# Streaming expert weights in chunks of 2 MB instead of 1 MB, with four neighbouring rows to a partition

## The reference, cut to what matters

```python
def moe(x, w_router, b_router, w1, w3, w2):      # x: 256 tokens x 1024
    e_idx, gates = route(xf, w_router, b_router) # 2 of 16 experts for each token
    ...
    def expert_block(args):
        xb, e = args
        hb = jax.nn.silu(xb @ w1[e]) * (xb @ w3[e])   # w1, w3: 1024 x 1024
        return hb @ w2[e]                             # w2: 1024 x 1024
    ...
    out = jnp.zeros((t, d), x.dtype).at[tok_s].add(y) # weighted by the gate
```

## Time and profile before

| | us |
|---|---|
| median of 3 runs | 2483.45 (2482.26 to 2487.23) |
| the profiled execution, its time | 2489.44 |
| its span | 2487.8 |
| first layer of experts, first product to last | 178.7 to 613.0 |
| second layer of experts, first product to last | 783.1 to 1217.4 |

### The profile page before, as it was taken

The page is one execution under the profiler, slowest core; times in us unless marked ns, Lnnn a source line. Parts: engine busy times, 40 slices in busy tenths (PEclk is TensorE's granted clock), DMA queues, the critical chain, the costliest instruction groups (busy, mean ns, idle before and its releaser), DMA issues.

```text
span 2487.8 us, 30159 instructions
## 1 busy us (share of the span) xinstructions
PE 2232.2 (90%) x12373; PEld 1559.5 (63%) x12373; DVE 955.8 (38%) x1217; ACT 719.6 (29%) x896; POOL 68.1 (3%) x78
## 2 busy tenths in 40 slices
PE   8869999997866999999599987979989998897998
PEld 6544334332754343333299976769979997676998
DVE  4741000001673000000345557645545546754554
ACT  4621000001451000000333344243343334424332
POOL 2000000000000000000100010000000001000000
PEclk9979999999987999999899989789999999968999
DMA  7189999999439999999955542045545554304551
GB/s 258 37 361 423 425 424 424 423 425 417 163 126 383 425 424 424 424 424 425 333 190 185 177 133 94 1 139 186 185 136 187 186 178 141 101 1 136 176 183 64
DMA packets 194676, 618.56 MB, mean 249 GB/s; under 512 B 10360, under 2 KB 119040, under 8 KB 145408
## 3 DMA queue, kind: packets, MB, share of 16 engines
q1 hardware_dynamic: 192416, 612.01, 64.6%
q0 software_dynamic: 2144, 4.94, 0.8%
HBM read 615.86 MB, written 1.05 MB: 248 GB/s over the span
## 4 chain that ended last, share of the span: by engine, by line
PE 72%; DMA 12%; DVE 8%; ACT 3%; DVEq 2%; issue 2%; ACTq 0%; SPq 0%
PE W L1730 18%; PE W L1892 7%; PE W L1893 7%; PE W L1894 7%; DMA moe_own<-in_moe_w 5%; DMA moe_split<-in_moe_w 5%; PE acc L1620 4%; PE acc L1621 4%; PE acc L1624 4%; PE W L1585 4%; PE W L1586 4%; PE W L1587 4%; PE W L1714 2%; DMA moe_xt<-in_moe_w 2%; PE acc L1723 2%
## 5 line engine op out<-in xcount | busy, mean ns | idle before, releaser
L977 DVE TENSOR_TENSOR w_lo<-raw,w_hi 128x2048 fp32r<-128x2048 f32 (+2 forms) x216 | 466.6, 2163 | 473.4 <-ACT w_hi L633 472.0
L633 ACT ACTIVATE w_hi<-raw 128x2048 fp32r<-128x2048 f32 (+2 forms) x216 | 382.3, 1772 | 595.6 <-PE W L1894 320.6
L1892 PE MATMUL W<-xT_hi,w_hi 128*128 128x256 f32 x1408 | 401.2, 285 | 7.5 <-DVE xT_lo L997 7.5
L1893 PE MATMUL W<-xT_lo,w_hi 128*128 128x256 f32 x1408 | 400.6, 285 | 0.0
L1894 PE MATMUL W<-xT_hi,w_lo 128*128 128x256 f32 x1408 | 400.5, 284 | 0.0
L1228 DVE TENSOR_TENSOR hid<-W,hid 128x512 f32<-128x512 f32 x32 | 22.1, 692 | 735.6 <-PE W L1730 735.6
L1892 PEld LDWEIGHTS W<-xT_hi,w_hi 128*128 128x128 f32 x1408 | 270.2, 192 | 10.3 <-DVE xT_lo L997 8.9
L1893 PEld LDWEIGHTS W<-xT_lo,w_hi 128*128 128x128 f32 x1408 | 270.2, 192 | 1.6
L1894 PEld LDWEIGHTS W<-xT_hi,w_lo 128*128 128x128 f32 x1408 | 270.3, 192 | 0.0
L1585 PE MATMUL W<-w_hi,xT_hi 128*128 128x474 f32 (+1 forms) x400 | 155.3, 388 | 9.9 <-DVE w_lo L977 4.8
L1730 PE MATMUL W<-moe_split,xe 128*64 128x512 f32 x672 | 153.2, 597 | 9.5 <-DMA moe_split<-in_moe_w 8.2
(11 more groups left out here) (334 smaller groups left out, 2743.9 us busy)
## 6 DMA issues: line engine op xcount, KB each, us to landing
moe_own<-in_moe_w SPq DMA_DIRECT2D x120, 1024.0 KB, 26.2
moe_split<-in_moe_w SPq DMA_DIRECT2D x120, 1024.0 KB, 26.2
raw<-in_moe_w SPq DMA_DIRECT2D x108, 1024.0 KB, 25.8
raw<-in_ffn_w_gate SPq DMA_DIRECT2D x44, 1024.0 KB, 5.3
raw<-in_ffn_w_up SPq DMA_DIRECT2D x44, 1024.0 KB, 5.3
raw<-in_ffn_w_down SPq DMA_DIRECT2D x44, 1024.0 KB, 4.9
moe_xt<-in_moe_w SPq DMA_DIRECT2D x36, 1024.0 KB, 26.0
raw<-in_w_in SPq DMA_DIRECT2D x32, 948.0 KB, 4.9
```

The source lines that it names most:

```text
L633: s.activation(w_hi[split_slot(c)][:, 0:cols], raw[slot_of(c)][:, 0:cols], ACT.Copy).then_inc(hi_ready, 1)
L977: v.tensor_tensor(w_lo[split_slot(c)][:, 0:cols], raw[slot_of(c)][:, 0:cols], w_hi[split_slot(c)][:, 0:cols].bitcast(F32), ALU.subtract).t ...
L1892: t.matmul(out, hi, xT_hi[:, kc, :], start=(kc == 0), stop=False)
L1893: t.matmul(out, hi, xT_lo[:, kc, :], start=False, stop=False)
```

## The change

A chunk becomes 2 MB: 512 rows of a matrix, partition p holding rows 4p to 4p+3, one run of 16 KB. An expert has 6 chunks, a layer 96. The ring has 10 slots of 16 KB a partition over the same bytes: 3 `moe_split`, 3 `moe_own`, 3 `moe_raw` (each over two neighbouring raw slots, so its fill waits for the later of the two) and 1 `moe_xt`. PE counts a chunk as used after 8 products (16 records) instead of 4. The stationary operands of the gather and of the hidden transposes now take every fourth column of `x` and `hid` (a step of 16 bytes). The counts for which ACT and DVE wait are those of the same points of the work. In the changed kernel the lines stand three (PE's part) or four (SP's part) further down.

```diff
-MOE_CHUNKS = 12
+MOE_ROWS = 4
+MOE_Q = KC // MOE_ROWS
+MOE_CHUNKS = 3 * MOE_Q
...
-MOE_OWN = 6
+MOE_OWN = 3
 MOE_SPLIT_AT = 0
-MOE_OWN_AT = MOE_SPLIT_AT + 2 * SPLIT_SLOTS
+MOE_OWN_AT = MOE_SPLIT_AT + SPLIT_SLOTS
 MOE_RAW_AT = MOE_OWN_AT + MOE_OWN
-MOE_XT_AT = MOE_RAW_AT + RAW_SLOTS
-MOE_SLOTS = MOE_XT_AT + 2
+MOE_XT_AT = MOE_RAW_AT + RAW_SLOTS // 2
+MOE_SLOTS = MOE_XT_AT + 1
...
         def raw_freed(layer, i):
-            slot = MOE_RAW_AT + i
+            slot = MOE_RAW_AT + i // 2
...
                 def fetch(m):
-                    e, i, q = m // MOE_CHUNKS, m % MOE_CHUNKS // 4, m % 4
+                    e, i, q = m // MOE_CHUNKS, m % MOE_CHUNKS // MOE_Q, m % MOE_Q
                     slot = m % MOE_SLOTS
-                    dst = moe_ring[slot][:].rearrange("p (k n) -> p k n", k=2)
-                    src = A[(...)[i]][layer, e, 256 * q:256 * (q + 1), :].rearrange("(p k) n -> p k n", k=2)
+                    dst = moe_ring[slot][:].rearrange("p (k n) -> p k n", k=MOE_ROWS)
+                    src = A[(...)[i]][layer, e, MOE_ROWS * P * q:MOE_ROWS * P * (q + 1), :].rearrange("(p k) n -> p k n", k=MOE_ROWS)
                     sp.dma_start(dst, src).then_inc(moe_landed[slot], 16)
...
-                        i = m - MOE_RAW_AT
-                        sp.wait_ge(lo_ready, c_end - (c_end - 1 - i) % RAW_SLOTS)
+                        sp.wait_ge(lo_ready, max(c_end - (c_end - 1 - i) % RAW_SLOTS for i in (2 * (m - MOE_RAW_AT), 2 * (m - MOE_RAW_AT) + 1)))
...
-            def every_second(a, kc):
-                return a[:, 256 * (kc // 2):256 * (kc // 2 + 1)].rearrange("p (c k) -> p k c", k=2)[:, kc % 2, :]
+            def every_fourth(a, kc):
+                return a[:, 512 * (kc // 4):512 * (kc // 4 + 1)].rearrange("p (c k) -> p k c", k=MOE_ROWS)[:, kc % 4, :]
...
-                        last = t.matmul(W[:, bank, j * P:(j + 1) * P].rearrange("p (a t) -> p a t", a=2), every_second(x[:, b], kc),
+                        last = t.matmul(W[:, bank, j * P:(j + 1) * P].rearrange("p (a t) -> p a t", a=2), every_fourth(x[:, b], kc),
...
-                    last = t.transpose(W[:, 0, k * P:(k + 1) * P], every_second(hid, k), ident[:])
+                    last = t.transpose(W[:, 0, k * P:(k + 1) * P], every_fourth(hid, k), ident[:])
...
-                    for k in range(2):
-                        last = halves(bank, stationary, 2 * q + k, moe_ring[m % MOE_SLOTS], k * D)
+                    for k in range(MOE_ROWS):
+                        last = halves(bank, stationary, MOE_ROWS * q + k, moe_ring[m % MOE_SLOTS], k * D)
                     return last.then_inc(moe_used, 1)
```

More of the change, by code:

```diff
@@ L162, in sem @@
             return ctx.enter_context(nc.semaphore(name))
+        raw_base = place[0]
         raw = [at(f"raw{i}", [P, SLOT]) for i in range(RAW_SLOTS)]
@@ L258, in build_program, with over @@
         count_max = at("count_max", [P, 1])
[L259 to L263, removed]
+        own = [at(f"moe_own{i}", [P, MOE_ROWS * D]) for i in range(MOE_OWN)]
+        def over(name, n, offset):
+            return [nc.alloc_sbuf_tensor_at(f"{name}{i}", [P, MOE_ROWS * D], F32, offset=offset + i * MOE_ROWS * D * 4) for i in range(n)]
+        moe_ring = over("moe_split", SPLIT_SLOTS, split_base) + own + over("moe_raw", RAW_SLOTS // 2, raw_base) + over("moe_xt", 1, xt_base)
         ov_raw = own[0][:, 0:D]
@@ L431, in fetch @@
                 def fetch(m):
-                    e, i, q = m // MOE_CHUNKS, m % MOE_CHUNKS // 4, m % 4
+                    e, i, q = m // MOE_CHUNKS, m % MOE_CHUNKS // MOE_Q, m % MOE_Q
                     slot = m % MOE_SLOTS
-                    dst = moe_ring[slot][:].rearrange("p (k n) -> p k n", k=2)
-                    src = A[("moe_w1", "moe_w3", "moe_w2")[i]][layer, e, 256 * q:256 * (q + 1), :].rearrange("(p k) n -> p k n", k=2)
+                    dst = moe_ring[slot][:].rearrange("p (k n) -> p k n", k=MOE_ROWS)
+                    src = A[("moe_w1", "moe_w3", "moe_w2")[i]][layer, e, MOE_ROWS * P * q:MOE_ROWS * P * (q + 1), :].rearrange("(p k) n -> p k n", k=MOE_ROWS)
                     sp.dma_start(dst, src).then_inc(moe_landed[slot], 16)
@@ L464, in more_rounds @@
                                     sp.wait_ge(o["free"], N(KC * i + kc + 1, (r, 24 * NE), (e, 24)).v)
-                                    pair = w[256 * (kc // 2):256 * (kc // 2 + 1), :].rearrange("(p k) n -> p k n", k=2)
-                                    sp.dma_start(ov_raw, pair[:, kc % 2, :]).then_inc(o["landed"], 16)
+                                    four = w[512 * (kc // 4):512 * (kc // 4 + 1), :].rearrange("(p k) n -> p k n", k=MOE_ROWS)
+                                    sp.dma_start(ov_raw, four[:, kc % 4, :]).then_inc(o["landed"], 16)
             def ffn(c0, l, which):
@@ L762, in experts @@
                     one = NE * layer + e + 1
-                    act.wait_ge(moe_used, MOE_LAYER * layer + MOE_CHUNKS * e + 4)
+                    act.wait_ge(moe_used, MOE_LAYER * layer + MOE_CHUNKS * e + MOE_Q)
                     s.activation(gated[:], W[:, 0, :], ACT.Silu).then_inc(me["sg"], 1)
@@ L1225, in experts @@
                         softplus()
-                    dve.wait_ge(moe_used, MOE_LAYER * layer + MOE_CHUNKS * e + 8)
+                    dve.wait_ge(moe_used, MOE_LAYER * layer + MOE_CHUNKS * e + 2 * MOE_Q)
                     dve.wait_ge(me["sg"], one)
@@ L1704, in gather @@
                     for b in range(TB):
-                        last = t.matmul(W[:, 3, kc * CAP:(kc + 1) * CAP], every_second(x[:, b], kc),
+                        last = t.matmul(W[:, 3, kc * CAP:(kc + 1) * CAP], every_fourth(x[:, b], kc),
                                         chosen_tokens[:, b, 0:CAP], start=(b == 0), stop=(b == TB - 1))
@@ L1792, in experts @@
                     tokens = xe[e // 2 % 2][:, :, CAP * (e % 2):CAP * (e % 2 + 1)]
-                    for q in range(4):
+                    for q in range(MOE_Q):
                         chunk(m + q, 0, tokens, q)
@@ L1796, in experts @@
                             add_expert(e - 1)
-                    for q in range(4):
-                        chunk(m + 4 + q, 1, tokens, q)
+                    for q in range(MOE_Q):
+                        chunk(m + MOE_Q + q, 1, tokens, q)
                     if e + 2 < NE:
@@ L1807, in experts @@
                     pe.wait_ge(me["hT"], one)
-                    for q in range(4):
-                        chunk(m + 8 + q, 2, heT, q)
+                    for q in range(MOE_Q):
+                        chunk(m + 2 * MOE_Q + q, 2, heT, q)
                 add_expert(NE - 1)
```

## The result

| | before | after |
|---|---|---|
| median of 5 runs, us | 2487.23 | 2504.99 |
| lowest and highest, us | 2482.26, 2491.25 | 2504.41, 2513.08 |
| profiled execution, its time and span | 2489.44, 2487.8 | 2513.08, 2511.5 |
| first expert layer, first gather to last product | 171.80 to 612.99 = 441.2 | 173.77 to 623.81 = 450.0 |
| second expert layer, the same | 776.30 to 1217.44 = 441.1 | 785.67 to 1235.72 = 450.0 |

The change makes the kernel slower: the ratio is 1.0081, 95% interval 1.006 to 1.0103, which is +20 us (+15 to +26). The two expert layers give 8.9 us each, 17.8 in sum. That is also the difference of the medians. The profiled execution itself is 23.6 us above that of before; the 6 us that are left lie outside the expert layers, 5.4 of them behind the second one, where the program is the same; runs of one kernel scatter by that much.

The account below looks back on a forecast made before the run. Transfers bound the expert layers, PE having 20.5 us of slack. PE's path, 592.5 + 26.7 = 619.2 us, would overtake them and end 6.2 us later a layer; 2483.45 + 12.4 = 2496 us, range 2473 to 2511.

Parts of the forecast that it names:

- The cadence of an expert: Time from expert to expert in the first third of a layer: 28.0 us if the step costs, 26.2 otherwise.
- The load: PE's load of 128 stationary columns at a step of 16 bytes: 0.218 us, against 0.130 a gather record now.
- The transposes: Hidden-value transposes on PE at a step of 16 bytes: 0.218 instead of 0.120 us each, +6.3 us a layer.
- The first gather: The 32 records before expert 0, 0.195 us each now at the lower clock: +0.7 us a layer.
- PE's slack: Time PE's own path would end before the transfers in an expert layer: 20.5 us in the first, 20.6 in the second.
- (a) First refill: SP's first ring refill after PE starts waits for 8 more records: +1.75 us a layer on the transfer path.
- (b) Last chunk: After a layer's last chunk lands PE has 16 records left instead of 8: +1.75 us a layer.
- (c) Fill: Raw slots filled in pairs put 2.5 us more work into 4 idle microseconds: 0, at most 1 us.
- (d) The rate: 16 KB packets instead of 8 KB in expert-layer transfers save 0.040 us a MB: -6.8 us a layer, 431 GB/s.
- Rival C: Step free and transfer rate unchanged, perhaps because 16 KB runs are cut again: +7 us in sum, 2490.5 us; chance 0.12.
- Rival B: Step free or nearly, load under 0.19 us, slack hides it, transfers decide: -6.6 us in sum, 2477 us; chance 0.28.
- D: Engines reading 16 KB runs hit the memory worse; at 2% rate lost +12 us a layer, 2507 us; chance 0.05.

Follow-up runs that it names:

- experiment 3: Kernel before plus float32 products and transposes at various stationary steps behind its end; one run: loads 0.116 us apart at 8 bytes, 0.232 at 16.
- experiment 2: The change with two 8 KB runs a partition in each 2 MB chunk, operands kept at every second column; median 2494.06 us, ratio 1.0021.
- experiment 7: experiment 5 with the first refill issued in two halves and a layer's last chunk in two transfers; median 2484.71 us, ratio 0.9992.
- experiment 8: experiment 7 with only the first 128 tokens' x copied, the other 128 gathered at a step of 16 bytes; median 2486.56 us, ratio 1.0009.
- experiment 5: The change with ACT copying x contiguous for the gather, layer-norm weights (1 MB) loaded only after the last gather; 2485.05 us, ratio 0.999.
- experiment 4: Kernel before plus float32r products and float32 ones with other moving lengths behind its end; one run: 512 columns 0.43 us at 4 and 16 bytes.

## Why the prediction was right, and where its terms were off

The forecast was that PE's path, lengthened by the step of 16 bytes, overtakes the transfers: +6.2 us a layer, 2496 us. It came so, with +8.9 us a layer and 2504.99 us. The path and the operand that lengthens it were right; that the load's size came out so near was in part luck, as it was taken from another engine's row with a step of 1 KB. By its own steps:

- **The cadence of an expert** was forecast at 28.0 us and is 28.08, but two errors cancel in it. **The load** was put at 0.218 us from DVE's 1.70 ns a value; by itself it takes 0.232 (experiment 3), and in the gather a record takes 3.93/16 = 0.246; both are 0.116 above their value at 8 bytes (0.116 and 0.130). The gathers in the loop cost 14 x 1.85 = 25.9 us instead of 19.7. **The transposes** were given 6.3 us and cost nothing: 0.48 us for 4 in both kernels. That term was wrong in kind, although the operand has the same step.
- **The first gather**: 7.75 - 6.25 = +1.5 us, forecast +0.7.
- **PE's slack** was put at 20.5 us and is 18.4. (Its sum takes 7.2 us for the last w2 where 32 x 0.22 is 7.0; measured are 7.11.) I took the two experts without a gather at 26.23 - 2.08 = 24.15 us; in the changed kernel, where PE never waits for a chunk, they take 616.70 - 591.49 = 25.21 us. Without the gather, DVE's product lies open: 0.78 us in which PE is idle, time that the gather covers otherwise, and the four transposes behind it take 0.76 us in the chain of waits instead of 0.48. That makes 1.06 us each. So 1.5 + 25.9 - 18.4 = 9.0 us, against 8.9 measured. These three terms are the whole difference between 6.2 and 8.9.
- **(a) First refill**: +1.75 forecast, 3.70 - 1.98 = +1.72 in experiment 2. **(b) Last chunk**: +1.75 forecast, 3.68 - 1.96 = +1.72. The layers there are 3.0 us longer instead of 3.5; the half microsecond lies between the first refill and the last landing, 429.67 us instead of 430.33, and its cause is open. **(c) Fill** cost nothing there: it was done before the first refill was issued (the DMA share is 0.21 in 180 to 185 us). What the step missed is that w3's last chunk sets nearly the same end, which experiment 7 showed.
- **(d) The rate**: 431 GB/s forecast, 429 to 430 measured; (2.473 - 2.441)/4 = 0.008 us a packet instead of 0.0099, 5.5 us a layer instead of 6.8. In the change it bought nothing, because the transfers were no longer what ended.
- **Rival C's doubt** that the run is cut again: the 24696 packets say no. **Rival B** wanted a load under 0.19 us and did not get it; experiment 8 makes its case by hand, with 14 us on PE's path and no loss against experiment 7. Its gain of 3.3 us a layer no run shows; experiment 5 less the 2.7 us of the late load would come to 439.4 us, an estimate of -1.8. **D** did not come.

The Trainium skill, SBUF — State Buffer, section "Door 1: The DMA port swizzle", gives both a need for two accesses to a 16-byte line and a free step of four float32 values. For the operands of a product the first half agrees with this chip, as 0.116 us at 8 bytes and 0.232 at 16 show; the second does not, except for transposes.

## What to carry to other kernels

A layout chosen for longer DMA runs also sets the step in which the matrix engine reads its operands. Weigh the two on their own paths: 1.3% of rate was worth 5.5 us, the step 27 us. A slow load of the stationary operand is free under 512 moving columns and shows in full under 128 (experiments 3 and 4). Where an engine first runs ahead and later waits, its slack is the sum of the later waits, but measure it with the idle that the hidden work covers; and count every megabyte that a rearrangement moves from an idle time of the DMA engines into a full one.

## What the runs showed of the hardware

- Stationary operand of 128 columns, 128 moving, float32 at full clock: loads 0.116 us apart at steps of 4 and 8 bytes, 0.17 at 12, 0.23 to 0.24 at 16 and 32, 0.22 at 64. Float32r at 12 bytes: 0.17. A moving operand at 16 bytes: 0.22 instead of 0.11 us.
- The load at 16 bytes takes 0.23 us at a granted clock of 1.00 and of 0.50 alike; at 12 bytes float32r goes from 0.17 to 0.21 us.
- A transpose of the same operand pays for none of these steps (0.12 us). The cause is open.
- HBM to SBUF with full engines: 387 GB/s with runs of 2 KB, 424 with 8 KB, 429 to 430 with 16 KB; the size of the transfer (1 or 2 MB at 8 KB) makes no difference.
- 1 MB more while PE waits for transfers: 2.7 us, a little over its 2.5 us of transfer.
